# Keys and values of an encoder layer as one 512-column weight panel instead of two of 256

## What is computed

```python
h = rms_norm(x, norm_mix_g)
z = h @ w_in                                   # w_in: 1024 x (u 1024, v 1024, q 1024, k 256, va 256, gates 2048)
u, v, q, k, va, gate_a, gate_b = jnp.split(z, SPLITS, axis=-1)
yb = window_attention(q, k, va, q_norm_g, k_norm_g, sink) @ w_proj_b    # 8 query heads, 2 key/value heads of 128
merged = jax.nn.sigmoid(gate_a) * ya + jax.nn.sigmoid(gate_b) * yb
x = x + merged @ w_out
x = x + hierarchical_moe(rms_norm(x, norm_ffn_g), ...)                  # top 2 of 32 experts
```

## Time and profile before

| what | value |
|---|---|
| time, median of 3 runs | 2108.15 us (2106.62 to 2111.38) |
| span of the profiled execution (the page gives no other time of it) | 2107.0 us |
| PE busy | 2078.6 us, 99% |
| DVE, ACT, POOL busy | 1297.7, 1072.7, 486.4 us |
| granted PE clock, mean | 0.996 |

### The profile page before, as it was taken

How to read it: one execution, slowest core, us unless ns; L and a number is a source line. 1 busy time by engine, 2 the same in 40 slices (tenths; PEclk the granted TensorE clock), 3 DMA queues, 4 the chain that set the end, 5 groups by cost and what they waited for, 6 DMA issues and landing times.

```text
span 2107.0 us, 30548 instructions
## 1 busy us (share of the span) xinstructions
PE 2078.6 (99%) x10380; PEld 1746.2 (83%) x10380; DVE 1297.7 (62%) x1687; ACT 1072.7 (51%) x1584; POOL 486.4 (23%) x656
## 2 busy tenths in 40 slices
PE   8999999999999999999999999999999999999997
PEld 7898888888888888898988888757888888887886
DVE  6664233465655233456653434369999999988995
ACT  5452333243542332345523232137888888877884
POOL 4252011210451011203510102011212222422321
PEclk9999999999999999999999999999999999999999
DMA  8213323443223322452122225487998789999892
GB/s 238 89 41 113 90 80 100 146 164 101 61 64 110 100 80 90 165 175 71 46 86 90 80 90 192 178 334 268 374 385 299 244 315 336 381 371 369 289 344 65
DMA packets 108739, 380.00 MB, mean 180 GB/s; under 512 B 13522, under 2 KB 19843, under 8 KB 83044
## 3 DMA queue, kind: packets, MB, share of 16 engines
q1 hardware_dynamic: 91812, 335.64, 44.4%
q0 software_dynamic: 16832, 43.08, 7.6%
HBM read 403.31 MB, written 34.60 MB: 208 GB/s over the span
## 4 chain that ended last, share of the span: by engine, by line
PE 51%; DMA 3%; DVE 1%; ACT 1%; issue 1%; POOL 0%; POOLq 0%; ACTq 0%; SPq 0%; DVEq 0%
PE main L552 3%; PE main L551 3%; PE main L550 3%; PE main L2059 3%; PE main L2061 3%; PE main L2060 3%; PE aux L2045 3%; PE main L2047 3%; DMA held_wu<-w_up_e 3%; PE main L2045 3%; PE main L2046 3%; PE aux L2047 3%; PE aux L2046 3%; PE main L538 2%; PE main L540 2%; PE main L539 2%
## 5 line engine op out<-in xcount | busy, mean ns | idle before, releaser
L1006 DVE TENSOR_TENSOR w_lo<-raw,w_hi 128x1024 fp32r<-128x1024 f32 (+1 forms) x216 | 250.8, 1182 | 270.9 <-ACT w_hi L750 270.8
L750 ACT ACTIVATE w_hi<-raw 128x1024 fp32r<-128x1024 f32 (+1 forms) x216 | 211.4, 1005 | 139.1 <-PE main L552 71.6
L550 PE MATMUL main<-e_g_hi,w_hi 128*128 128x512 f32 x576 | 235.5, 409 | 0.0
L552 PE MATMUL main<-e_g_hi,w_lo 128*128 128x512 f32 x576 | 225.8, 392 | 0.0
L551 PE MATMUL main<-e_g_lo,w_hi 128*128 128x512 f32 x576 | 225.3, 391 | 0.0
L2188 DVE TENSOR_TENSOR e_d_lo<-held_wd,e_d_hi 128x2048 fp32r<-128x2048 f32 x76 | 173.6, 2287 | 54.1 <-ACT e_d_hi L2117 54.0
L538 PE MATMUL main<-w_hi,e_g_hi 128*128 128x512 f32 (+1 forms) x560 | 203.5, 363 | 0.6 <-DVE e_g_lo L1020 0.6
L540 PE MATMUL main<-w_hi,e_g_lo 128*128 128x512 f32 (+1 forms) x560 | 200.2, 357 | 0.0
L539 PE MATMUL main<-w_lo,e_g_hi 128*128 128x512 f32 (+1 forms) x560 | 200.0, 357 | 0.0
L2188 DVE TENSOR_TENSOR e_u_lo<-held_wu,e_u_hi 128x2048 fp32r<-128x2048 f32 x76 | 173.3, 2282 | 14.0 <-ACT e_u_hi L2117 14.0
L2188 DVE TENSOR_TENSOR e_g_lo<-held_wg,e_g_hi 128x2048 fp32r<-128x2048 f32 x76 | 173.5, 2283 | 1.4 <-ACT e_g_hi L2117 1.2
(11 more groups left out here) (368 smaller groups left out, 4730.1 us busy)
## 6 DMA issues: line engine op xcount, KB each, us to landing
held_wg<-w_gate_e SPq DMA_DIRECT2D x78, 1024.0 KB
held_wu<-w_up_e SPq DMA_DIRECT2D x78, 1024.0 KB
held_wd<-w_down_e SPq DMA_DIRECT2D x76, 1024.0 KB
raw<-w_in SPq DMA_DIRECT2D x120, 512.0 KB, 3.8
raw<-w_proj_b SPq DMA_DIRECT2D x24, 512.0 KB, 3.8
raw<-w_proj_a SPq DMA_DIRECT2D x24, 512.0 KB, 3.9
raw<-w_out SPq DMA_DIRECT2D x24, 512.0 KB, 4.5
raw<-w_in SPq DMA_DIRECT2D x24, 256.0 KB, 4.8
```

Of the source, the lines that this page charges most:

```text
L550: pe.matmul(bank[:], hi[:, k, :], mov_hi[:, k, :], start=(k == 0), stop=False)
L552: mm = pe.matmul(bank[:], lo[:, k, :], mov_hi[:, k, :], start=False, stop=(k == KT - 1))
L750: act.activation(hi, buf, ACT.Copy).then_inc(w_hi_done, 1)
L1006: dve.tensor_tensor(lo, buf, hi.bitcast(F32), ALU.subtract).then_inc(w_split, 1)
```

## The change

Keys and values become one panel of 512 columns, `PKV`. There are 17 panels for each group instead of 18. Since 17 is odd, the buffer of a panel now depends on the group (`weights_at`). All that was done in the value panel moves: the value copy stands ahead of the squares of the same tile, the turning of `ws` and the last `route_logits` go to the first query panel, `nsink` too. The halo tile is one tile of 24 matmuls in one bank instead of two. All four quarters of the first panel are full size, so quarter 3 has no half buffer to go to: its load waits for the split of quarter 0. `h2T` gets a second place for tiles 2 and 3 of a group, because the values are written into `va`, on which it lies, one panel earlier.

```diff
-PANELS = [("w_in", K0, 256), ("w_in", VA0, 256), ("w_in", Q0, 512), ("w_in", Q0 + 512, 512),
+PANELS = [("w_in", K0, 512), ("w_in", Q0, 512), ("w_in", Q0 + 512, 512),
...
-PK, PVA, PQ, PGB, PPB, PV, PU, PGA, PPA, POUT = 0, 1, 2, 4, 6, 8, 10, 12, 14, 16
+PKV, PQ, PGB, PPB, PV, PU, PGA, PPA, POUT = 0, 1, 3, 5, 7, 9, 11, 13, 15
...
+def weights_at(g, p):
+
+    return (g * NP + p) % 2
...
-        at = 512 if i == 3 else 0
-        buf = raw[i % NRAW][:, at:at + 2 * n].rearrange("p (k c) -> p k c", k=2)
-        return src, buf, w_hi[p % 2][:, 2 * q:2 * q + 2, 0:n], w_lo[p % 2][:, 2 * q:2 * q + 2, 0:n]
+        b = i // NQ % 2
+        buf = raw[i % NRAW].rearrange("p (k c) -> p k c", k=2)
+        return src, buf, w_hi[b][:, 2 * q:2 * q + 2, :], w_lo[b][:, 2 * q:2 * q + 2, :]
...
-        return h2, h2T, (aux[2], aux[3])
+        return h2, h2T_late if t >= 2 and g < NG - 1 else h2T, (aux[2], aux[3])
...
         load_quarter(2)
-        load_quarter(3)
         load_x(1)
         load_x(2)
         load_x(3)
-        for i in range(1, NG * QPG - NRAW):
-            sp.wait_ge(w_split, 4 if i == 3 else i + 1)
+        for i in range(NG * QPG - NRAW):
+            sp.wait_ge(w_split, i + 1)
             load_quarter(i + NRAW)
...
-            if p in (PK, PQ, PQ + 1):
-                n = head_at(g, None if p == PK else p - PQ, j)
-                return (head_squared, n), (head_read, n)
-            if p == PVA:
-                return (va_done, kv_at(g, j)),
+            if p in (PKV, PQ, PQ + 1):
+                n = head_at(g, None if p == PKV else p - PQ, j)
+                kept = ((va_done, kv_at(g, j)),) if p == PKV else ()
+                return ((head_squared, n), (head_read, n)) + kept
...
-                    if g == 0 and p == PVA and 1 <= j <= 2:
+                    if g == 0 and p == PQ and 1 <= j <= 2:
                         transpose_ws(j - 1)
...
-                    if g and p == PVA and first:
+                    if g and p == PQ and first:
                         route_logits(g - 1, 3)
...
-                    if p == PK:
+                    if p == PKV:
+                        copy_va(g, j, main[j])
                         square_heads(head_at(g, None, j), main[j], NKV, lambda k: ssk[:, j, k:k + 1])
-                    if p == PVA:
-                        copy_va(g, j, main[j])
```

More of the change, by code:

```diff
@@ L79, in tiles_of, with half_of @@
 def tiles_of(g, p):
-    return [j for j in range(GT) if p not in (PK, PVA) or j in KV_TILES[g]]
+    return [j for j in range(GT) if p != PKV or j in KV_TILES[g]]
+def half_of(p):
+    return (p - PQ) % 2
+def weights_at(g, p):
+    return (g * NP + p) % 2
 LAST = [(POUT, 0), (POUT, 1), (POUT + 1, 0), (POUT, 2), (POUT + 1, 1), (POUT, 3), (POUT + 1, 2), (POUT + 1, 3)]
@@ L186, in mixers @@
     h2T = place("h2T", [P, KT, P], F32, at["va"] + 2048)
+    h2T_late = place("h2T_late", [P, KT, P], F32, at["A"] + 8192)
     rA, B, C, Dd, T1, T2 = (at[name] for name in ("A", "B", "C", "D", "T1", "T2"))
@@ L262, in sem @@
         return ctx.enter_context(nc.semaphore(name))
-    raw_in, fourth_in = [sem(f"raw_in{i}") for i in range(NRAW)], sem("fourth_in")
+    raw_in = [sem(f"raw_in{i}") for i in range(NRAW)]
     w_hi_done, w_split, out_ready = sem("w_hi_done"), sem("w_split"), sem("out_ready")
@@ L529, in transpose_ws, with token_major @@
             mm.then_inc(ws_ps, 1)
-        def token_major(bank, stat_hi, stat_lo, p, ready=None):
-            n = PANELS[p][2]
-            hi, lo = w_hi[p % 2], w_lo[p % 2]
+        def token_major(g, bank, stat_hi, stat_lo, p, ready=None):
+            hi, lo = w_hi[weights_at(g, p)], w_lo[weights_at(g, p)]
             for k in range(KT):
@@ L537, in token_major @@
                     ready(k)
-                pe.matmul(bank[:, 0:n], stat_hi(k), hi[:, k, 0:n], start=(k == 0), stop=False)
-                pe.matmul(bank[:, 0:n], stat_hi(k), lo[:, k, 0:n], start=False, stop=False)
-                mm = pe.matmul(bank[:, 0:n], stat_lo(k), hi[:, k, 0:n], start=False, stop=(k == KT - 1))
+                pe.matmul(bank[:], stat_hi(k), hi[:, k, :], start=(k == 0), stop=False)
+                pe.matmul(bank[:], stat_hi(k), lo[:, k, :], start=False, stop=False)
+                mm = pe.matmul(bank[:], stat_lo(k), hi[:, k, :], start=False, stop=(k == KT - 1))
             return mm
@@ L646, in ready @@
                             pe.wait_ge(a_done if p == PPA else m_done, KT * g + k + 1)
-                    if g == 0 and p == PK:
+                    if g == 0 and p == PKV:
                         if j == 0:
@@ L691, in tensor @@
                             transpose_h(g + 1, sl - 4)
-                    if g and p == PK:
+                    if g and p == PKV:
                         i = KV_TILES[g].index(j)
@@ L720, in tensor @@
                     mm.then_inc(out_ready, 1)
[L721 to L728 removed]
+                if g == 1 and p == PKV and j == 3:
+                    pe.wait_ge(hx_done, 2)
+                    n = head_at(1, None, HALO)
+                    bank = take(0, (head_squared, n), (head_read, n), (va_done, kv_at(1, HALO)))
+                    token_major(1, bank, lambda k: hx_hi[:, k, :], lambda k: hx_lo[:, k, :], p).then_inc(halo_ready, 1)
         route_logits(NG - 1, 1)
@@ L784, in copy_h2T @@
             act.wait_ge(h2_ps, 2 * n + 1)
-            if to is h2T:
+            if to is not h2T_last:
                 act.wait_ge(l_ps, n)
@@ L869, in copy_va @@
                 act.wait_ge(halo_kept, 1)
-            act.activation(va[:, t + 1, :], bank[:, 0:256], ACT.Copy).then_inc(va_done, 1)
+            act.activation(va[:, t + 1, :], bank[:, 256:512], ACT.Copy).then_inc(va_done, 1)
         def round_a(g, c):
@@ L914, in scalar @@
                         continue
-                    if g and p == PK and j in KV_TILES[g]:
+                    if g and p == PKV and j in KV_TILES[g]:
                         i = KV_TILES[g].index(j)
@@ L1343, in vector @@
                     elif p < POUT and p not in (PGB, PGB + 1):
-                        if g == 0 and p == PVA and j == 3:
+                        if g == 0 and p == PQ and j == 0:
                             gain_k_tile(HALO)
@@ L1448, in vector @@
                         dve.tensor_tensor(r, main[sl % 4][:], r, ALU.add).then_inc(x2_done, 1)
-                if p == PK and j == 3:
+                if p == PKV and j == 3:
                     if g == 1:
```

63 lines of the change are left out of this document (26 added, 37 removed).

## The result

| | us | against before |
|---|---|---|
| before, median (runs of the same occasion) | 2107.2 | |
| after, median of 6 runs | 2119.3 (2117.4 to 2122.6) | ratio 1.0060, 95% interval 1.0049 to 1.0070 |
| predicted | 2111.2, range 2106.8 to 2115.0 | |
| span of the profiled execution | 2117.5 (before 2107.0) | +10.5 |

The change costs 12 us of 2107, nearly three times the 4.2 us that the prediction takes as the least a measurement can tell, and the time lies outside the range.

What follows compares the result with a forecast made beforehand. It took PE's pitch in all groups, and ACT with the first transfers in group 0, as the bound; +4.9 + 0.7 − 1.6 − 0.9 = +3.1 on 2108.15 gave 2111.2 us, range 2106.8 to 2115.0.

Steps and rivals of the forecast that it cites:

- Costed at nothing: Wider first-panel splits of groups 1 and 2, POOL's late loads, value copies: taken as covered; splits otherwise 1.3 us, twice.
- What bounds the kernel: PE's matmul pitch in all groups; in group 0 also the start, set by ACT and the first transfers.
- Matmuls: Key and value matmuls, 576 narrow become 288 wide: gains 1.6 us in group 1 and 0.9 in group 2.
- The start: Group 0: fourth quarter lands at 18.0 us, first key matmul 21.2, first query matmul 48.3 instead of 43.33; loss 4.9 us.
- Rival B: Start of group 0: fourth quarter lands still later, each us adding one; at 20.5 the total is 2113.8; chance 0.27.
- The turning of ws: Two sets of four transposes, 0.36 us each, move from value panel to first query panel: +0.7 us.
- Rival C: Between groups: h2T copy of groups 0 and 1 comes 1 to 2 us late, +2 to +4, about 2114; chance 0.07.
- POOL's late loads: Group 0: loads waiting for key statistics move some 17 us, landing at 69, covered by 2 us before their first reader.

Runs made afterwards that it cites:

- Run 7: Kernel before, with the first three quarters of the next group's key panel issued only once x tile 3 has landed; 2103.7 us, −3.7 against before.
- run 6: Changed kernel with start order turned, later groups' fourth split behind the last hidden tile, next group's quarters held until x tile 3 landed; 2105.2 us.
- run 9: Changed kernel: fourth quarter early in own buffer, gain row's copy ahead, later fourth splits behind last hidden tile, next quarters held until x tile 3 landed; 2102.4 us.
- run 10: Run 6's kernel with the last group's residual loads of x waiting until two quarters of the last panel are split; 2104.5 us, −3.7 against before.
- run 11: Run 9's kernel plus run 10's edit, the last group's residual loads behind the last quarter, on the wide panel; 2100.2 us, −6.6 against before.
- run 3: Changed kernel with only the split of the next group's fourth quarter moved behind the last hidden tile's rounding; 2117.4 us, +8.9 against before.
- Run 5: Changed kernel with the first three quarters of the next group's panel issued only once x tile 3 has landed; 2112.9 us, +5.5 against before.
- run 1: Changed kernel with the first panel's fourth quarter in a buffer of its own, issued ahead of the x tiles; 2113.6 us, +5.1 against before.
- run 2: Changed kernel, same loads, but second hidden half, x tile 1's square and norm, and gain row's copy ahead of the fourth quarter's split; 2113.5 us.
- run 4: Changed kernel with key and value tiles of groups 1 and 2 computed in two passes of 256 columns over the wide panel; 2120.9 us.
- run 8: Kernel before with only the first panel's fourth quarter (256 KB) issued behind x tiles 1 to 3; 2115.8 us, +8.4 against before.

## Why the prediction was wrong

The step that failed is "Costed at nothing". With the landing of the fourth quarter as it came (20.05 us instead of 18.0) the sum would have been 2113.3, inside the range. What took the time out of it lies at the groups' ends and between them, priced at nothing: +1.31, +1.75, +1.04 and +0.60 in the table, 4.7 us, and 1.69 us at the low clock inside group 1.

**What bounds the kernel: right.** TensorE's own pitch inside the groups, ScalarE and the transfers at the start. It stopped one step short: the kernel before had two waits at the groups' ends (1.41 and 1.21 us), and no step asked what made them. Run 7 shows that it was x landing late beside the next group's quarters.

**Matmuls: right.** Predicted gains were 1.6 and 0.9 us. Group 2's stage gave back 0.82 to 0.89. Group 1's gave 0.15, because 1.69 us at the low clock lie in it. A wide tile lasts 5.5 us (503.69 to the turning at 509.26 is 5.57), as predicted. The Trainium skill ("TensorE: Matmul & The Clock Gate", section "Wait — 56ns, not 53.3ns?") gives a fixed 2.5 ns for each matmul; an estimate from it is 0.06 us for 24 pairs. The traces don't agree: the measured 0.29 a tile is 12 ns a pair. The stage of group 2, priced at 0.9 us, was 0.8 us shorter in every trace with wide matmuls. (An estimate by that rule is 0.2.) Group 1's, where nothing disturbs it (runs 6, 9, 10 and 11), takes 41.07 us from route_logits of tile 1 to that same turning of keys, the narrow one 42.62 to 43.10: 1.6 to 2.0 for the 1.6 predicted.

**The start: right mechanism, one term mis-sized.** "I take 18.0" for the landing of the fourth quarter: it was 20.05, outside the upper bound of 18.65. In the six further runs with that order of loads on the wide panel the split began between 19.6 and 20.3, so it is no accident. The chain from split to first matmul was predicted at 3.2 us and took 3.16, the stage from first key to first query matmul at 27.1 and took 27.3. The bound failed because it paid the extra 0.79 MB at the 360 GB/s of a window in which the engines were full. Here full engines did not mean that rate: from 14 to 16 us they were full at 150 GB/s, with small pieces of another queue. At 360 GB/s those 2 us would have moved 0.42 MB more, which is 1.2 of the 1.4 us beyond the bound. That is worked out from the rows; no run moved GpSimd's loads. Rival B was this, at 0.27.

**The turning of ws: right,** 0.87 us for 0.7.

**"Costed at nothing", the widened splits between groups: wrong.** The prediction added up the chain to 454.9 us, "just covered, and I take that", with 1.3 us twice as its other end. The wait came (1.58 and 0.43 us), and run 3 shows that the order of the splits makes it. Three things were left out of the price:
- The chain named in the prediction was right in kind and wrong at its end. It looked at the copy of h2T; the work behind that copy, the rounding of the last hidden tile, is what frees the bank of route_logits, and it ended 1.8 us after the copy in the kernel before (454.01 for 452.21). The delay itself was priced well: 2.7 us predicted, and the copy came 2.9 later than the 9.44 us already lost by the group's end (464.01 for 451.63). Those 2.9 on the right end, 454.01, give 456.95, which is 1.6 us behind 455.31; the wait was 1.58.
- The quarters of the next group cross the x tiles at a group's end. Twice the bytes moved x tile 3 and through it the norms and the turning of xn and h2 (in the table +1.31, and +1.04 of which 0.46 is a wait for w_lo). The prediction counted the wider transfer only in the quarter that waits for it. Run 5 shows 4.06 us of waits gone, part of which the kernel before had too.
- The clock fell behind the wait, so it cost twice: 1.58 us of wait, and 1.69 of low clock.

Rival C was the nearest to what happened between the groups (+2 to +4), at a chance of 0.07, and taken as an alternative to B. Both came together. That is the error in the chances: the cases were priced as if one excluded the others, and the sum of B and C, about 2117, stood nowhere.

**POOL's late loads: covered, as costed.** The last one was issued at 60.52 and landed 7.9 us later, at 68.4 (predicted 69), and no wait of TensorE or VectorE in group 0 leads to them.

**What stays open.** The last group's wait for w_lo, 1.45 us where the kernel before has 0.25, is the landing of the last panel's fourth quarter, 9.0 us instead of 7.8 after its issue, with the same issues around it. It was 1.1 to 1.6 us in the traces of runs 1, 2, 3, 5, 6 and 9, which have wide matmuls, and 0 to 0.3 in those of runs 4, 7 and 8 and of before, which have narrow ones. No row here shows how the width of the key and value matmuls could reach a transfer some 370 us later. Shorter waits for w_lo of the same panel also come and go at the ends of groups 0 and 1 (0.43 to 0.85 us in the traces of the changed kernel and of runs 1, 2, 3, 6, 9 and 11). Run 10 removes the last group's wait; it does not explain the two landings. The 2.6 us that the changed kernel makes good after 1357 us are in part shorter stretches at the low clock (granted 0.98 from 1350 to 1450 us and 0.96 from 2050 to the end, where the kernel before has 0.97 and 0.95 ten us earlier), which differ between executions; no experiment was made on them.

## What to carry to other kernels

Making a block of weights larger changes three things at once: the matmuls that read it, the place of its last part in the queue of transfers, and how much traffic crosses other loads at the stage's edge. Price the second and third with the engines' share and the rate apart, and look behind a late transfer for everything that is queued after its consumer: here most of a 10 us wait was for work that needed none of the late data (run 2). A wait that exists before the change has a cause; find it, since the change may feed it, and if it doesn't, removing it is a gain of its own (3.7 us here for two lines).

## What the runs showed of the hardware

- **Full transfer engines at 150 GB/s.** 45 packets of GpSimd's queue with 0.05 MB took 61.5% of the engines' time from 14 to 16 us, while from 12 to 14 us full engines (share 1.12) moved 380 GB/s. It is one stretch of one kernel, and no run took those packets away.
- **The clock after short waits.** With TensorE busy at the full clock for hundreds of us, waits of 1.3 to 1.9 us next to transposes or thin matmuls were followed in some executions by 3 to 4 us at a granted clock near 0.5 and in others not: behind 1.92 us at 442.96 of the changed kernel the clock stayed, behind 1.89 us at the same place of run 1 it fell. In front of route_logits it fell behind 1.58 us (changed kernel) and 1.45 (run 5), and stayed behind 1.49 (run 1). So the price of one and the same wait was 1.9 or 3.5 us.
- **The clock can fall without a wait.** In the kernel before, 32 matmuls of 4 columns take 3.6 us from 1194.22, without a wait, and the clock is down from 1198.7 to 1202.1. In run 1 it stayed down for some 7 us at the same place, in runs 4 and 5 it did not fall there at all. Rows of the kernel before:

```profile
1198.00:1200.00 2.00, 2.00 (x7) 1.53 (x6) 0.89 (x3) 0.63 (x1) 0.34 (x1) 0.69 0.65 227
1200.00:1202.00 2.00, 2.00 (x6) 1.61 (x5) 0.00 (x0) 0.00 (x0) 0.00 (x0) 0.50 0.00 0
```

- **At the start the record of the granted clock can differ from the pitch.** In the changed kernel it says 1.00 from 22 to 28 us while matmuls start 0.427 us apart, the pitch of 512 columns at 1.2 GHz; in run 3, with the same start, it says 0.50. There the pitch is what tells.
